# Gated-delta recurrence: inverse and its turned form in PSUM banks of their own, and row sums of exponents in two split passes

## The chip, the cores and the metric

The kernel runs on one core of a Trainium2 chip. The metric is the device time of one execution in microseconds (us), the median of three runs.

## What is computed

One layer of a streaming encoder with three groups of mixing heads (window attention, gated delta rule, stick-breaking attention) and a feed-forward part, for a prompt of 2048 tokens and eight samples of 16 tokens. What matters here is the gated delta rule, six heads of width 64, in chunks of 64 tokens:

```python
gc = jnp.cumsum(g, axis=-1)
decay = jnp.exp(jnp.where(causal, gc[..., :, None] - gc[..., None, :], NEG))
kb = k * beta
lower = jnp.where(strict, jnp.einsum("...id,...jd->...ij", kb, k) * decay, 0.0)
rhs = jnp.concatenate([v * beta, kb * jnp.exp(gc)[..., None]], -1)
sol = lax.linalg.triangular_solve(lower + jnp.eye(chunk), rhs, left_side=True, lower=True, unit_diagonal=True)
u, w = sol[..., :dv], sol[..., dv:]
intra = jnp.where(causal, jnp.einsum("...id,...jd->...ij", q, k) * decay, 0.0)
...
v_new = u_i - w_i @ s
o = (q_i * jnp.exp(gc_i)) @ s + a_i @ v_new
s = s * jnp.exp(g_last) + (k_i * jnp.exp(g_last - gc_i)).T @ v_new
```

## The kernel before

The program runs its stages one after the other: front, window attention, recurrence (stage_delta), stick-breaking attention, mixing, feed-forward. Each stage gives every engine one instruction stream, written out by hand in its order, and engines meet only at semaphores. The order of the calls in each engine's loop is therefore the order of the work; nothing reorders it.

stage_delta handles 17 tiles of 128 tokens: tile 0 holds the samples, tiles 1 to 16 the prompt, two chunks each on the two halves of the partitions. The loop variable k counts turns. In turn k tile k is inverted, tile k-1 is solved and applied to the state, tile k+1 is prepared, and the output of tile k-2 is turned and stored. SP loads tiles four ahead (load), and stores.

The triangular solve is an inverse by doubling. POOL multiplies mats by level masks (mask_L, first_masks, later_masks) into L, and writes X_1, the inverse at the first level. PE's first_inverse(k) brings it into PSUM by products with the identity, once straight (a = 0) and once turned (a = 1); ps_X has two banks, and each holds three heads, both forms side by side. inverse_copied takes bank 0 to SBUF on DVE and bank 1 on ACT. Each level l then has lower_times_inverse (L times X into ps_Y, copied to Y by ACT in product_copied) and add_to_inverse (X times Y, added in ps_X). Levels run to 5, for tile 0 to 3. The last level needs only the turned form, XT, which solved() uses. Between these steps the PE stream has work of the other tiles: solved, kv_rows, from_state, into_state, exponents, products, norms_and_sums, turn_out.

Preparation of tile k+1: norms_and_sums on PE (twelve matmuls with two columns and a few with six), factor_logs on DVE (small 128x6 operations, result fac_log), factors on ACT, log_diag on POOL (identity times a row of fac_log, into diag), kv_rows on PE with scale_kv on DVE, then per half exponents on PE: seq_sum times diag, 384 columns of fp32, plus a mask product in bf16; weights on ACT takes the exponential, products on PE and matrices on DVE give mats.

DVE's loop in turn k: inverse_copied(k, 0), factor_logs(k+1), inverse_copied(k, 1), scale_kv(k+1), squares_summed, inverse_copied(k, 2), state_updated, normalised, decays(k+2), inverse_copied(k, 3), matrices(k+1, 0), inverse_copied(k, 4), state_updated, matrices(k+1, 1), inverse_copied(k, 5), output(k-1). POOL's: later_masks(k), soften(k+2), log_diag(k+1), gates, square(k+2), in turn 0 sample_operands, first_masks(k+1), squared_and_gated(k-1). ACT's begins: inverse_copied(k, 0), product_copied(k, 1), wT_copied(k-1), factors(k+1), inverse_copied(k, 1).

Names and tensors of the trace: d_inverse is X, d_inverse_T is XT, d_inverse_first X_1, d_LX is Y, d_minus_L is L, d_log_diag is diag, ps_d_prepared is ps_P. All products of the doubling have line L2623, that of the helper quadrants. An fp32 matmul stands as two records, so twelve matmuls of a quadrants call over three heads (or one call over six) show as x12 (or x24).

At the start of the stage DVE sets three large tiles to zero, then signals blank_ready, on which SP loads the sample states and after them load(2) and load(3). Before the loop, DVE runs decays(0), factor_logs(0), scale_kv(0), matrices(0, 0) and (0, 1), decays(1).

## Time and profile before

| what | value |
| --- | --- |
| median of 3 runs | 3658.67 us (3653.52 to 3665.99) |
| the profiled execution | 3662.05 us |
| its span | 3660.6 us |
| mean granted clock of TensorE | 0.959 |
| PE busy | 3386.8 us, 93% |
| PEld busy | 3029.3 us, 83% |
| DVE busy | 2121.3 us, 58% |
| ACT busy | 1451.0 us, 40% |
| POOL busy | 390.7 us, 11% |

The profiled execution is one run with the hardware profiler on, and its span is the time from its first to its last instruction. The shares are averages over stages with different limits, so the stage of the change must be looked at by itself: it lies in slices 10 to 16 of the page's 40. PE is TensorE, PEld its weight loads, DVE VectorE, ACT ScalarE, POOL GpSimd, SP SyncE. A granted clock of 1.00 is 2.4 GHz and 0.5 is 1.2 GHz.

### The profile page before, as it was taken

What the parts mean: (1) busy time and instruction counts of PE and PEld (TensorE: products, weight loads), DVE (VectorE), ACT (ScalarE), POOL (GpSimd) and SP (SyncE); (2) the same over time, 40 slices, a digit from 0 to 9 for tenths busy, and PEclk for the clock granted to TensorE, in tenths of its full rate; (3) what the DMA queues carried; (4) which work ended last, traced back from release to release, by engine and by line L of the source; (5) the groups of instructions that cost most, each with busy time, mean ns of one, the idle gap of its engine ahead of it and who ended that gap; (6) DMA issues with size and microseconds to landing.
All of it is one profiled execution on the core that took longest, in us unless ns stands there. A gap on an engine that the chain in (4) does not pass through costs nothing. (4 is left out here: it accounts for less than half of the span.)

```text
span 3660.6 us, 68507 instructions
## 1 busy us (share of the span) xinstructions
PE 3386.8 (93%) x27409; PEld 3029.3 (83%) x27409; DVE 2121.3 (58%) x3584; ACT 1451.0 (40%) x2716; POOL 390.7 (11%) x582
## 2 busy tenths in 40 slices
PE   7999999876999996996599599999999999999997
PEld 7899999854888884664488599899899899899895
DVE  2656556664444444773488465575575575575695
ACT  2434444452344443663334243343343343343353
POOL 0000000022444441000023100000000000000000
PEclk8999999987999998998899799999999999999999
DMA  7677756632011103007666645455455455455464
GB/s 221 176 223 224 224 171 188 189 116 64 22 35 36 45 18 115 7 7 269 203 200 214 191 127 161 128 161 161 128 161 161 128 161 161 128 161 149 143 192 129
DMA packets 706413, 521.55 MB, mean 142 GB/s; under 512 B 64649, under 2 KB 650616, under 8 KB 706044
## 3 DMA queue, kind: packets, MB, share of 16 engines
q1 hardware_dynamic: 659400, 429.25, 39.8%
q0 software_dynamic: 26576, 70.12, 5.6%
q10 hardware_dynamic: 20128, 17.83, 1.6%
q8 instruction: 222, 3.64, 0.4%
q14 instruction: 87, 0.70, 0.1%
HBM read 432.11 MB, written 86.05 MB: 142 GB/s over the span
## 5 line engine op out<-in xcount | busy, mean ns | idle before, releaser
L1219 PE MATMUL ps_gate_up<-h2T_group_high,w_gate_up_high 128*128 128x384 f32 (+1 forms) x2112 | 689.5, 326 | 22.1 <-DVE w_gate_up_low L1315 16.2
L1220 PE MATMUL ps_gate_up<-h2T_group_low,w_gate_up_high 128*128 128x384 f32 (+1 forms) x2112 | 688.6, 326 | 0.0
L1221 PE MATMUL ps_gate_up<-h2T_group_high,w_gate_up_low 128*128 128x384 f32 (+1 forms) x2112 | 688.6, 326 | 0.0
L1219 PEld LDWEIGHTS ps_gate_up<-h2T_group_high,w_gate_up_high 128*128 128x128 f32 x2112 | 398.8, 189 | 24.7 <-issue 24.6
L1220 PEld LDWEIGHTS ps_gate_up<-h2T_group_low,w_gate_up_high 128*128 128x128 f32 x2112 | 398.8, 189 | 0.0
L1221 PEld LDWEIGHTS ps_gate_up<-h2T_group_high,w_gate_up_low 128*128 128x128 f32 x2112 | 398.8, 189 | 0.0
L1315 DVE TENSOR_TENSOR w_gate_up_low<-w_gate_up,w_gate_up_high 128x1024 fp32r<-128x1024 f32 x264 | 322.3, 1222 | 62.2 <-ACT w_gate_up_high L1253 51.7
L1321 DVE TENSOR_TENSOR w_down_low<-w_down_ring,w_down_high 128x512 fp32r<-128x512 f32 x264 | 182.3, 693 | 290.6 <-ACT w_down_high L1259 290.5
L1253 ACT ACTIVATE w_gate_up_high<-w_gate_up 128x1024 fp32r<-128x1024 f32 x264 | 279.3, 1058 | 159.2 <-PE ps_gate_up L1221 135.1
L1259 ACT ACTIVATE w_down_high<-w_down_ring 128x512 fp32r<-128x512 f32 x264 | 166.0, 631 | 331.4 <-PE ps_down L1231 169.3
L433 PE MATMUL ps_feature<-hT_high,w_in_high 128*128 128x384 f32 (+1 forms) x816 | 271.6, 333 | 9.7 <-DVE hT_low L607 8.4
L435 PE MATMUL ps_feature<-hT_high,w_in_low 128*128 128x384 f32 (+1 forms) x816 | 266.6, 327 | 0.0
L434 PE MATMUL ps_feature<-hT_low,w_in_high 128*128 128x384 f32 (+1 forms) x816 | 266.5, 327 | 0.0
L581 DVE TENSOR_TENSOR w_in_low<-w_in_ring,w_in_high 128x1024 fp32r<-128x1024 f32 (+1 forms) x150 | 170.1, 1140 | 125.2 <-ACT w_in_high L497 125.2
L1231 PE MATMUL ps_down<-w_down_high,hidden_high 128*128 128x512 f32 x506 | 199.6, 394 | 4.4 <-DVE w_down_low L1321 2.0
L497 ACT ACTIVATE w_in_high<-w_in_ring 128x1024 fp32r<-128x1024 f32 (+1 forms) x150 | 148.5, 990 | 137.3 <-PE ps_token L453 91.7
L1231 PE MATMUL ps_down<-w_down_low,hidden_high 128*128 128x512 f32 x506 | 197.2, 390 | 0.0
L1231 PE MATMUL ps_down<-w_down_high,hidden_low 128*128 128x512 f32 x506 | 197.2, 390 | 0.0
L1270 ACT ACTIVATE gate_raw<-ps_gate_up 128x384 f32<-128x384 f32 (+1 forms) x132 | 60.0, 455 | 319.5 <-PE ps_gate_up L1221 319.5
L433 PEld LDWEIGHTS ps_feature<-hT_high,w_in_high 128*128 128x128 f32 x816 | 154.5, 189 | 14.3 <-issue 12.4
L1358 DVE SCALAR_TENSOR_TENSOR gated_down<-gate_raw,ffn_taps,gated_down 128x384 f32<-128x384 f32 (+1 forms) x264 | 151.7, 575 | 21.2 <-issue 1.7
L434 PEld LDWEIGHTS ps_feature<-hT_low,w_in_high 128*128 128x128 f32 x816 | 154.5, 189 | 0.0
(437 smaller groups left out, 6681.3 us busy)
## 6 DMA issues: line engine op xcount, KB each, us to landing
w_gate_up<-in_w_gate SPq DMA_DIRECT2D x132, 512.0 KB, 3.7
w_gate_up<-in_w_up SPq DMA_DIRECT2D x132, 512.0 KB, 3.7
w_down_ring<-in_w_down SPq DMA_DIRECT2D x264, 256.0 KB, 2.8
w_in_ring<-in_w_in SPq DMA_DIRECT2D x84, 512.0 KB, 4.2
w_ada_ring<-in_w_ada SPq DMA_DIRECT2D x48, 512.0 KB, 5.3
s_ck_rows<-in_cache_c_k SPq DMA_DIRECT2D x32, 512.0 KB, 7.8
s_cv_rows<-in_cache_c_v SPq DMA_DIRECT2D x32, 512.0 KB, 7.5
d_convT<-scratch_convT SPq DMA_DIRECT2D x17, 576.0 KB, 4.3
```

Of the source, the lines that this page charges most:

```text
L433: pe.matmul(out, high[:, cols], h_high, start=(k == 0), stop=False)
L434: pe.matmul(out, high[:, cols], h_low, start=False, stop=False)
L435: last = pe.matmul(out, low[:, cols], h_high, start=False, stop=(k == DC - 1))
L581: dve.tensor_tensor(w_low[:, u % SPLIT, 0:width], w[:, u % RAW, 0:width], w_high[:, u % SPLIT, 0:width].bitcast(F32), ALU.subtract).then_i ...
L1219: pe.matmul(out, w_high, h_high, start=(k == 0), stop=False)
L1220: pe.matmul(out, w_high, h_low, start=False, stop=False)
L1221: last = pe.matmul(out, w_low, h_high, start=False, stop=(k == DC - 1))
L1231: last = pe.matmul(down_bank(half, t), h[:, c, tok], w[:, j % WR], start=(c == 0 and part == 0), stop=(c == FC - 1 and part == 2))
L1253: act.activation(flat(wgu_high[:, c % 2, j]), flat(wgu[:, c % 2, j]), ACT.Identity).then_inc(s[f"high_ready{j}"], 1)
L1259: act.activation(wd_high[:, j % WR], wd[:, j % WD], ACT.Identity).then_inc(s["wd_high_ready"], 1)
L1315: dve.tensor_tensor(flat(wgu_low[:, c % 2, j]), flat(wgu[:, c % 2, j]), flat(wgu_high[:, c % 2, j]).bitcast(F32), ALU.subtract).then_inc(s ...
L1321: dve.tensor_tensor(wd_low[:, j % WR], wd[:, j % WD], wd_high[:, j % WR].bitcast(F32), ALU.subtract).then_inc(s["wd_split"], 1)
```

## The change

Each bank of ps_X now holds one form for all six heads: bank 0 the inverse, which DVE copies to X, and bank 1 the turned form, which ACT copies to X_T (XT at the last level). PE waits for DVE's copy alone before L times X. For tiles from 1 on the first doubling issues only the products that give the straight form; the turned form is X_1 itself, which ACT copies into bank 1 (inverse_begun) and which add_to_inverse reads at level 1. DVE's copy at the last level is gone. The row sums of the exponents run as two fp32r products over high and low parts: ACT rounds two rows of fac_log (rows_rounded), DVE subtracts (row_low, at the end of factor_logs), POOL makes both diagonals (eight operations instead of four). DVE's three large memsets move from the stage's begin to behind decays(1); SP waits for load(0) before load(1).

```diff
--- before.py
+++ after.py
@@ -2385,13 +2385,14 @@
     GATE = {0: slice(0, H), 1: slice(H, 2 * H)}
-    BETA, KBE, KD, QG = range(4)
+    QG, KBE, BETA, KD = range(4)
...
         half_size = lambda name, shape: ctx.enter_context(nc.sbuf_tensor(name, shape, BF16))
+        sb_r = lambda name, shape: ctx.enter_context(nc.sbuf_tensor(name, shape, F32R))
...
         decay = sb("d_decay", [P, LATE, DEC_B, J])
-        diag = sb("d_log_diag", [P, H, 2, C])
+        row_high, row_low = sb_r("d_row_logs_high", [P, 2, H]), sb("d_row_logs_low", [P, 2, H])
+        diag_high, diag_low = (sb_r(f"d_log_diag_{n}", [P, H, 2, C]) for n in ("high", "low"))
+        seq_sum_r = sb_r("d_seq_sum", [P, P])
...
         X_1 = sb("d_inverse_first", [P, H, C])
-        X, XT = sb("d_inverse", [P, H, 2, C]), sb("d_inverse_T", [P, H, C])
+        X, X_T, XT = (sb(f"d_inverse{n}", [P, H, C]) for n in ("", "_turning", "_T"))
...
                              "squares_ready soft_in_ready soft_ready g_ready norms_done logs_ready sums_done fac_log_ready "
-                             "fac_ready diag_ready kv_done kv_ready G_done wgt_ready qk_done mats_ready L_ready X_1_ready "
+                             "fac_ready row_high_ready rows_split diag_ready kv_done kv_ready G_done wgt_ready qk_done mats_ready L_ready X_1_ready base_ready "
...
         Y_base = lambda n: 0 if n == 0 else 3 + 5 * (n - 1)
-        X_base = lambda n: Y_base(n) + n
...
             load(0)
+            sp.wait_ge(loaded[0], 32)
...
             def log_diag(n):
-                pool.wait_ge(s["fac_log_ready"], n + 1)
+                pool.wait_ge(s["rows_split"], n + 1)
...
                 for half in range(2):
-                    for a, f in enumerate((QG, KBE)):
-                        row = fac_log[:, f].rearrange("p (j a) -> p a j", a=2)[:, half]
-                        last = pool.tensor_tensor(diag[:, halves[half], a, :], ident[:].unsqueeze(1).to_broadcast([P, J, C]),
-                                                  row.unsqueeze(2).to_broadcast([P, J, C]), ALU.mult)
+                    for diag, rows in ((diag_high, row_high[:].bitcast(F32)), (diag_low, row_low[:])):
+                        for a in range(2):
+                            row = rows[:, a].rearrange("p (j a) -> p a j", a=2)[:, half]
+                            last = pool.tensor_tensor(diag[:, halves[half], a, :], ident[:].unsqueeze(1).to_broadcast([P, J, C]),
+                                                      row.unsqueeze(2).to_broadcast([P, J, C]), ALU.mult)
...
                 if n:
-                    for half in range(2):
-                        pool.wait_ge(s[f"Z_done{half}"], X_base(n - 1) + 1)
+                    pool.wait_ge(s["Z_done1"], Y_base(n - 1) + 1)
...
             def sample_operands():
+                pool.wait_ge(s["blank_ready"], 1)
...
             square(1)
-            pool.wait_ge(s["blank_ready"], 1)
...
         def _(pe):
-            def quadrants(outs, lhs, rhs, heads, first, stop):
-                for i in heads:
+            def quadrants(bank, lhs, rhs, first):
+                for i in range(H):
...
                         r = rows_of[c]
-                        last = pe.matmul(outs(r, i), lhs(r, i), rhs(r, i), start=first and i == heads[0], stop=stop,
+                        last = pe.matmul(bank[r, i * C:(i + 1) * C], lhs(r, i), rhs(r, i), start=first and i == 0, stop=True,
...
                 return last
-
-            def heads_of(half):
-                return range(half * J, half * J + J)
-
-            def inverse_at(a):
-                return lambda r, i: ps_X[r, i // J, i % J * 2 * C + a * C:i % J * 2 * C + (a + 1) * C]
...
                     pe.wait_ge(s["mats_ready"], 2 * n + 1)
-                pe.matmul(ps_P[:, 0:W], seq_sum[:, 0, :], flat(diag[:, halves[half]]), start=True, stop=True)
+                pe.matmul(ps_P[:, 0:W], seq_sum_r[:], flat(diag_high[:, halves[half]]), start=True, stop=False)
+                pe.matmul(ps_P[:, 0:W], seq_sum_r[:], flat(diag_low[:, halves[half]]), start=False, stop=True)
...
                 pe.wait_ge(s["X_1_ready"], n + 1)
-                for half in range(2):
-                    if n:
-                        pe.wait_ge(s[f"X_ready{half}"], X_base(n))
-                    quadrants(inverse_at(1), lambda r, i: K["ident"][r, r], lambda r, i: X_1[r, i, :], heads_of(half), True, True)
-                    quadrants(inverse_at(0), lambda r, i: X_1[r, i, :], lambda r, i: K["ident"][r, r], heads_of(half), False, True
-                              ).then_inc(s[f"Z_done{half}"], 1)
+                if n:
+                    pe.wait_ge(s["X_ready0"], Y_base(n))
+                quadrants(ps_X[:, 0], lambda r, i: X_1[r, i, :], lambda r, i: K["ident"][r, r], True).then_inc(s["Z_done0"], 1)
+                if n == 0:
+                    quadrants(ps_X[:, 1], lambda r, i: K["ident"][r, r], lambda r, i: X_1[r, i, :], True)
...
                 pe.wait_ge(s["L_ready"], Y_base(n) + l)
-                for half in range(2):
-                    pe.wait_ge(s[f"X_ready{half}"], X_base(n) + l)
-                    last = quadrants(lambda r, i: ps_Y[r, i * C:(i + 1) * C], lambda r, i: L[r, l, i, :],
-                                     lambda r, i: X[r, i, 0, :], heads_of(half), half == 0, True)
-                last.then_inc(s["Y_done"], 1)
+                pe.wait_ge(s["X_ready0"], Y_base(n) + l)
+                quadrants(ps_Y, lambda r, i: L[r, l, i, :], lambda r, i: X[r, i, :], True).then_inc(s["Y_done"], 1)
...
             def add_to_inverse(n, l):
+                turned = X_1 if l == 1 else X_T
                 pe.wait_ge(s["Y_ready"], Y_base(n) + l)
-                for half in range(2):
-                    if l < last_level(n):
-                        quadrants(inverse_at(0), lambda r, i: X[r, i, 1, :], lambda r, i: Y[r, i, :], heads_of(half), False, True)
-                    quadrants(inverse_at(1), lambda r, i: Y[r, i, :], lambda r, i: X[r, i, 1, :], heads_of(half), False, True
-                              ).then_inc(s[f"Z_done{half}"], 1)
+                if l == 1:
+                    if n:
+                        pe.wait_ge(s["base_ready"], n)
+                else:
+                    pe.wait_ge(s["X_ready1"], Y_base(n) + l - 1)
+                if l < last_level(n):
+                    quadrants(ps_X[:, 0], lambda r, i: turned[r, i, :], lambda r, i: Y[r, i, :], False).then_inc(s["Z_done0"], 1)
+                quadrants(ps_X[:, 1], lambda r, i: Y[r, i, :], lambda r, i: turned[r, i, :], False).then_inc(s["Z_done1"], 1)
...
             def solved(n):
-                for half in range(2):
-                    pe.wait_ge(s[f"X_ready{half}"], X_base(n) + last_level(n) + 1)
+                pe.wait_ge(s["X_ready1"], Y_base(n) + last_level(n))
...
 
+            def rows_rounded(n):
+                act.wait_ge(s["fac_log_ready"], n + 1)
+                act.activation(row_high[:], fac_log[:, QG:KBE + 1], ACT.Identity).then_inc(s["row_high_ready"], 1)
+
+            def inverse_begun(n):
+                act.wait_ge(s["X_1_ready"], n + 1)
+                act.wait_ge(s["X_ready1"], Y_base(n))
+                act.activation(ps_X[:, 1, 0:W], X_1[:].rearrange("p h c -> p (h c)"), ACT.Identity).then_inc(s["base_ready"], 1)
+
             def inverse_copied(n, l):
-                act.wait_ge(s["Z_done1"], X_base(n) + l + 1)
-                if l < last_level(n):
-                    last = act.activation(flat(X[:, halves[1]]), ps_X[:, 1, 0:W], ACT.Identity)
-                else:
-                    last = act.activation(XT[:, halves[1]], ps_X[:, 1, 0:W].rearrange("p (h a c) -> p h a c", a=2, c=C)[:, :, 1],
-                                          ACT.Identity)
-                last.then_inc(s["X_ready1"], 1)
+                act.wait_ge(s["Z_done1"], Y_base(n) + l)
+                dst = X_T if l < last_level(n) else XT
+                act.activation(dst[:].rearrange("p h c -> p (h c)"), ps_X[:, 1, 0:W], ACT.Identity).then_inc(s["X_ready1"], 1)
...
             norm_logs(0)
+            rows_rounded(0)
...
                 solving, preparing = exists(k - 1) and not sample(k - 1), exists(k + 1)
-                if exists(k):
-                    inverse_copied(k, 0)
+                if exists(k) and k:
+                    inverse_begun(k)
...
                 if preparing:
+                    rows_rounded(k + 1)
...
         def _(dve):
-            for t in (s_state, s_wT, s_qT):
-                last = dve.memset(t[:], 0.0)
             dve.memset(sums[:], 0.0)
-            dve.drain()
-            dve.sem_inc(s["blank_ready"], 1)
+            dve.tensor_copy(seq_sum_r[:], seq_sum[:, 0])
...
                 dve.tensor_tensor(fac_log[:, KD], minus_gc[:], whole, ALU.add).then_inc(s["fac_log_ready"], 1)
+                dve.wait_ge(s["row_high_ready"], n + 1)
+                dve.tensor_tensor(row_low[:], fac_log[:, QG:KBE + 1], row_high[:].bitcast(F32), ALU.subtract
+                                  ).then_inc(s["rows_split"], 1)
...
             def inverse_copied(n, l):
-                dve.wait_ge(s["Z_done0"], X_base(n) + l + 1)
-                if l < last_level(n):
-                    last = dve.tensor_copy(flat(X[:, halves[0]]), ps_X[:, 0, 0:W])
-                else:
-                    last = dve.tensor_copy(XT[:, halves[0]], ps_X[:, 0, 0:W].rearrange("p (h a c) -> p h a c", a=2, c=C)[:, :, 1])
-                last.then_inc(s["X_ready0"], 1)
+                dve.wait_ge(s["Z_done0"], Y_base(n) + l + 1)
+                dve.tensor_copy(X[:].rearrange("p h c -> p (h c)"), ps_X[:, 0, 0:W]).then_inc(s["X_ready0"], 1)
...
             decays(1)
+            for t in (s_state, s_wT, s_qT):
+                last = dve.memset(t[:], 0.0)
+            last.then_inc(s["blank_ready"], 1)
...
                     decays(k + 2)
-                if 3 in inverting:
+                if 3 in inverting and not sample(k):
...
                     matrices(k + 1, 1)
-                if 5 in inverting:
-                    inverse_copied(k, 5)
...
```

## Rows read from the trace of the kernel before

**Rows 1.** Busy time and records by engine, clock, DMA: steady part of the stage.

```profile
990.00:1384.00 394.00, 385.80 (x7729) 342.21 (x7728) 177.39 (x429) 164.51 (x479) 178.78 (x230) 0.95 0.12 33
```

**Rows 2.** Timeline of POOL, d_inverse_first: start us, us, engine, line, operation.

```profile
990.44 0.99 POOL L2559 TENSOR_TENSOR d_inverse_first<-d_minus_L,delta_ident 128x384 f32<-128x384 f32 x1 [0.20 <-issue]
...
1218.32 0.99 POOL L2559 TENSOR_TENSOR d_inverse_first<-d_minus_L,delta_ident 128x384 f32<-128x384 f32 x1 [0.20 <-issue]
...
1245.36 0.99 POOL L2559 TENSOR_TENSOR d_inverse_first<-d_minus_L,delta_ident 128x384 f32<-128x384 f32 x1 [0.20 <-issue]
...
1275.10 0.99 POOL L2559 TENSOR_TENSOR d_inverse_first<-d_minus_L,delta_ident 128x384 f32<-128x384 f32 x1 [0.20 <-issue]
```

**Rows 3.** Timeline of PE, from the first doubling of a full-clock turn to level 2.

```profile
1107.95 0.56 PE L2623 MATMUL ps_d_inverse<-d_inverse_first,const_ident 64*64 64x64 f32 x12
...
1109.62 1.04 PE L2623 MATMUL ps_d_LX<-d_inverse,d_minus_L 64*64 64x64 f32 x21
...
1111.61 0.52 PE L2623 MATMUL ps_d_inverse<-d_LX,d_inverse 64*64 64x64 f32 x12
...
1113.91 0.91 PE L2623 MATMUL ps_d_LX<-d_inverse,d_minus_L 64*64 64x64 f32 x24
```

**Rows 4.** Timeline of DVE, the same stretch.

```profile
1108.92 0.56 DVE L3094 COPY d_inverse<-ps_d_inverse 128x384 f32<-128x384 f32 x1 [0.22 <-PE ps_d_inverse L2623]
...
1110.58 0.96 DVE L3071 TENSOR_TENSOR d_minus_gc<-d_norm_logs,d_sums 128x6 f32<-128x6 f32 x1
...
1112.52 0.56 DVE L3094 COPY d_inverse<-ps_d_inverse 128x384 f32<-128x384 f32 x1
```

**Rows 5.** Timeline of POOL, the same turn.

```profile
1104.50 0.99 POOL L2549 TENSOR_TENSOR d_minus_L<-d_matrices,delta_level_T 128x384 f32<-128x384 f32 x1 [14.19 <-DVE d_matrices L3088]
...
1110.52 3.88 POOL L2549 TENSOR_TENSOR d_minus_L<-d_matrices,delta_level_T 128x384 f32<-128x384 f32 x4
```

**Rows 6.** Timeline of PE: row sums, fp32r products of another stage, an uncovered copy.

```profile
1092.32 0.86 PE L2623 MATMUL ps_d_LX<-d_inverse,d_minus_L 64*64 64x64 f32 x23
1093.11 0.91 PE L2668 MATMUL ps_d_prepared<-d_log_diag,delta_seq_sum 128*128 128x384 f32 x2
1093.86 0.33 PE L2669 MATMUL ps_d_prepared<-d_expo_mask_half,d_ident_half 128*128 128x384 bf16 x1
1094.12 0.56 PE L2623 MATMUL ps_d_inverse<-d_LX,d_inverse 64*64 64x64 f32 x12
...
2200.05 0.33 PE L1219 MATMUL ps_gate_up<-h2T_group_high,w_gate_up_high 128*128 128x384 f32 x1
2200.22 0.33 PE L1220 MATMUL ps_gate_up<-h2T_group_low,w_gate_up_high 128*128 128x384 f32 x1
...
900.68 0.92 PE L2623 MATMUL ps_d_LX<-d_inverse,d_minus_L 64*64 64x64 f32 x24
...
902.19 0.56 PE L2623 MATMUL ps_d_inverse<-d_LX,d_inverse 64*64 64x64 f32 x12 [0.59 <-ACT d_LX L2925]
```

**Rows 7.** Timeline of DVE, PE and POOL in the first turns; last row: DMA issues, to landing.

```profile
862.76 2.62 DVE L3026 MEMSET d_s_wT<- 128x3072 f32 x1 [0.59 <-issue]
...
870.45 2.69 PE L2638 MATMUL ps_d_prepared<-delta_in_seq,d_squares 128*128 128x2 f32 x12 [15.96 <-DVE d_expo_mask_half L3032]
...
867.56 0.20 POOL L2531 TENSOR_TENSOR d_soft_in<-d_zero,d_zba 128x6 f32<-128x6 f32 x1 [6.08 <-DMA d_norm_w<-in_b_norm_w]
...
875.89 1.91 POOL L2542 TENSOR_TENSOR d_log_diag<-delta_ident,d_factor_logs 128x192 f32<-128x192 f32 x4 [4.02 <-DVE d_factor_logs L3074]
...
894.72 0.20 POOL L2531 TENSOR_TENSOR d_soft_in<-d_zero,d_zba 128x6 f32<-128x6 f32 x1
...
895.16 0.56 DVE L3094 COPY d_inverse<-ps_d_inverse 128x384 f32<-128x384 f32 x1 [3.17 <-PE ps_d_inverse L2623]
...
d_convT<-scratch_convT SPq DMA_DIRECT2D x4, 576.0 KB, 6.3
...
921.18 0.91 PE L2623 MATMUL ps_d_inverse<-d_inverse_first,const_ident 64*64 64x64 f32 x12
```


## Prediction

> **What bounds the kernel now.** I read the page first and then the stages. The change lies in one stage, the gated-delta recurrence, which runs from about 859 to 1405 us. In the middle of it, the steady part, TensorE is busy 385.80 of 394 us and its mean granted clock is 0.95 [rows 1]. VectorE and ScalarE are under half busy there. So TensorE's queue sets the time, and the other engines matter where its next instruction waits for them. A busy TensorE here also covers short gaps, since the ends of matmuls are modelled, so I go by start times, not by busy time.
>
> One 128-token tile is one turn of the loop. The POOL instruction that writes d_inverse_first marks it. From 1218.32 to 1245.36 a turn takes 27.04 us. The next takes 29.74, and ten turns from 990.44 take 284.66, or 28.47 each [rows 2]. The difference of 1.43 us a turn is time at half clock (1.2 instead of 2.4 GHz); where TensorE runs the two-column norm matmuls just before, little streams through it. So there are two things to sum: the turn at full clock, and what the clock takes.
>
> **First doubling.** Before, first_inverse issues four groups of 12 matmul records, and now two (the identity products that wrote the turned form go). A group costs about 0.35 us: VectorE's copy starts when two groups from 1107.95 have started and the last record of 0.22 has ended, at 1108.92 (0.75 for two). So 0.70 us of TensorE's work goes. But the next step is a dependence. That copy starts 0.97 after the first matmul, and L times X begins at 1109.62 [rows 3, 4]. After the change the same 24 records come first, so VectorE starts at the same 0.97. Its copy of 0.56 and a hand-over of about 0.06 let L times X start at 1.6 instead of 1.67. What is left is that L times X no longer waits half-way for ScalarE's copy; the row at 1109.62 runs 1.04 us with 21 records, the one of level 3 at 1092.32 0.86 with 23 [rows 3, 6], so 0.18 and the 0.07, 0.25 us in all. So of 0.70 us of work removed, 0.45 becomes an idle gap, and add_to_inverse, at 1111.61 before, can start about 0.25 earlier.
>
> **The new wait behind it.** That 0.25 must pass VectorE. Its order is copy of X, the small factor_logs operations, copy of X for level 1. The last row shows that second copy at 1112.52 with no idle time before it: VectorE is late there already, TensorE's L times X of level 2 following at 1113.91 [rows 3, 4]. The change puts into that chain a round trip: fac_log to ScalarE (rows_rounded), back to VectorE (row_low), then only the copy. Queued behind row_low are the copy of X for level 1 and scale_kv; TensorE's level 2 waits for the copy. The trace of before has no such operation on ScalarE; the nearest row of that size is POOL's of 0.20 at 894.72 [rows 7], so with two hand-overs of 0.05 the trip costs 0.3, plus row_low (0.2 by the same row if undisturbed). But a VectorE subtraction of two SBUF tiles of this size takes 0.96 at 1110.58, while POOL runs mask products of 0.97 each (3.88 for four from 1110.52), and ends at 1111.54, about when the first of them does [rows 4, 5]. So row_low costs 0.2 to 1.0.
>
> The Trainium skill's page "SBUF — State Buffer", section "Who interferes with whom", says that a VectorE instruction with two SBUF inputs and a GpSimd instruction that reads SBUF exclude each other for a whole instruction. By that rule row_low costs a full product; without it the step would cost 0.5. The rows side with the rule.
>
> POOL itself moves. VectorE no longer copies at the last level, so output() need not wait for that level, and POOL goes from its first masks at 1104.50 straight on. Three products of 0.97, a pause between them, and the two 384-column products of the output are some 4.9 us, so the four later products start near 1109.4 instead of 1110.52 [rows 5] (an estimate). If VectorE's first small operation just gets in, row_low ends at about 1113.25, the copy at 1113.8, and level 2 starts at 1113.9: no gain, no loss. If it doesn't, the chain is one product later and level 2 starts at 1114.4: 0.5 lost. I take the middle, +0.25, in full-clock turns. In half-clock turns TensorE is slower than this chain and keeps what it is given: 0.4 (the first group of products takes twice the time, the idle gap doesn't). With eight and seven turns: +2.0 and -2.8 us.
>
> **Row sums.** One fp32 pass over 384 columns is two records, 0.75 us from start to start (1093.11 to 1093.86). An fp32r matmul of this shape starts 0.17 after the one before (2200.05, 2200.22) [rows 6]. Two of them and the change of form cost 0.35 to 0.4. So TensorE saves 0.35 to 0.4 per half. How much arrives depends on what the row sums covered: ScalarE's copy of LX. With nothing between, L times X at 900.68 is followed by add_to_inverse at 902.19: 1.51 us. Level 3 takes 1.80 now (1092.32 to 1094.12) [rows 6], so it can only fall by 0.29. Level 4's row sums start later behind L times X, for they wait for matrices(), so nearly all of TensorE's saving arrives there, an estimated 0.32. Sum 0.61 a turn (0.3 if ScalarE is late, 0.8 with no cover lost) for 15 turns: -9.0 us (-4.5 to -12).
>
> log_diag becomes eight POOL products instead of four, +1.91 us by its row [rows 7]. In a steady turn they follow the masks that end at 1114.4, so they end by 1118.8, and the next row sums start at 1093.11 + 27.04 = 1120.15; POOL has 14.19 idle us before 1104.50 to take the rest [rows 5, 6]. If that cover were gone each turn would pay up to 1.9. The added ScalarE copy of X_1 into PSUM (no row of before; about the 0.56 of VectorE's copy of that size, 0.3 to 0.7) runs between the mix copy and the LX copy, where ScalarE idles; it has no price. The full-width last copy on ScalarE is needed only by solved(), after L times X: no price.
>
> **The start.** Before, the three blanking memsets hold VectorE for 3.2 us each (2.62 and 0.59 idle, twice), TensorE waits for the masks that VectorE makes after them until 870.45, and POOL's first work at 867.56 waits for the norm row's load [rows 7]. With the memsets gone TensorE can follow the squares, 1.0 us earlier; with load(1) held back the row may land earlier too. That gain g is 1 to 4; I take 2. log_diag(0), 1.91 at 875.89, doubles and gets the round trip, 2.4 more; the key and value rows cover part of it, so +1.0 (0 to 2.4). The two row sums run at half clock there, where the 0.75 is 1.50 and the new pair 0.7 to 0.8: 0.7 less each. So matrices come 2.4 earlier. But the memsets now stand between decays(1) and the first copy of X, at 895.16 after 3.17 idle, so decays(1) ends at 891.99 [rows 7]. 891.99 less 2.4 plus 9.0 (three of 2.62, two pauses) is 898.6: +3.4. The same signal releases SP: state loads and load(2) are queued behind it, and POOL's soften(2), at 894.72 before, must wait for load(2). With 6.3 us from issue to landing [rows 7] and the state loads ahead, that is about 906. Behind it stand log_diag(1), square, sample_operands and the first masks of tile 1, whose doubling starts at 921.18 now. POOL is some 11 us late there. It had idle time of about that length later in the turn (it is busy 178.78 of 394 us in the steady part [rows 1]), so I don't add the two: the +3.4 less 0.6 for what the row sums save in this turn, +2.8 (-1 to +6).
>
> **The clock.** Nothing in the norms changes, and which turns are hit depends on how they fall. With an idle gap right behind and fewer columns streamed, I expect somewhat more of it: +3 us, from -5 to +19 (all 15 turns like the worst one, 2.70 instead of 1.43). The last two turns, without preparation, give -0.4.
>
> **Sum:** -9.0 +2.0 -2.8 +2.8 +3.0 -0.4 = -4.4 us. The profiled execution took 3662.05 (span 3660.6), 3.4 above the median of 3658.67, which is within the spread of the runs; against it the sum gives 3657.7, against the median 3654.3.
>
> **The rivals.**
> 1. The gain arrives in full (g near 4, VectorE's chain gets in before the masks, 0.8 a turn from the row sums): -12 for the row sums, -2.8 -2 for the doubling, -1 for the start, +0 clock: 3641. For it: the 0.8 and 0.70 us of work removed a turn are real, and TensorE bounds. Against: ScalarE's copy at 902.19. Chance 0.22.
> 2. The round trip takes the lock's place: each turn loses 0.5 and, at the start, load(2) holds POOL to the full (+6): 3654.3 + 2 + 3.2 + 2.8, about 3662. It decides if row_low ends after 1113.4 on the clock of that turn. For it: VectorE has no idle time before 1112.52. Chance 0.25.
> 3. Slower: the clock falls in every turn, between norms and first doubling, at 2.70 a turn. That is 19 us more than now in place of the 3: 3670. It exceeds the gain from about six more turns hit. For it: the gap is put just behind the thinnest stretch. Against: the transposes of turn_out stand between them. Chance 0.13. The Trainium skill's page "TensorE: Matmul & The Clock Gate", section "HAM oscillation — how this bites in real kernels", tells of idle gaps that send the clock down turn after turn; it would make this rival likelier, and the rows so far show falls only behind the norms.
>
> **How the numbers follow.** My forecast, 3654.3, has chance 0.40. A measurement of this kernel can tell about 0.3%, 11 us, from no change. Forecast and rival 2 fall inside that, rival 1 and 3 mostly outside. Faster by over 0.3%: 0.24; within: 0.61; slower: 0.15. The range takes in rival 1's and rival 3's near parts: 3640 to 3669.
>
> **What would show it.** First doubling to level 2, 5.96 us before (1107.95 to 1113.91): 5.7 to 6.5 after, with an idle gap of about 0.9 us on TensorE released by VectorE's copy. Row sums 0.4 instead of 0.75, and add_to_inverse of level 3 at 1.5 us behind L times X. A full-clock turn of 26.4 (26.0 to 26.9). The copy of X for level 0 of tile 0 near 898.6, POOL's soften(2) waiting for a load. If a full-clock turn is 27 or more, the round trip is mis-sized; if it is below 26, the covers are. If the stage's mean clock falls below 0.93, rival 3 holds.

## The result, and the profile after

The changed kernel takes 3695.21 us (median of 4 runs, 3694.63 to 3697.7) against 3662.33 for the kernel before on the same chip. The ratio is 1.0086, with a 95% interval from 1.0068 to 1.0103: slower by 0.9%, where 3654.3 was forecast, and outside the range of 3640 to 3669.

Its profiled execution has a span of 3693.9 us, 33.3 more than before. I cut both spans at four points that both traces have: the POOL instructions that write d_inverse_first for tiles 3 and 16, and the first gate product (L1219) of the last stage, the feed-forward network.

| stretch | before, us | after, us | difference |
| --- | --- | --- | --- |
| start of the span to tile 3 | 990.4 | 999.4 | +9.0 |
| tile 3 to tile 16 (13 turns) | 367.5 | 378.3 | +10.8 |
| tile 16 to the first gate product | 707.7 | 708.4 | +0.7 |
| first gate product to the end | 1594.9 | 1607.7 | +12.8 |

Three of the four grew by about the same. The last of them is a stage in which no line was changed. I take them in turn.

**The turns.** The windows of the steady part and of three parts of one turn (columns: window, its length, busy us and records of PE, PEld, DVE, ACT and POOL, granted clock, DMA share, GB/s):

```profile
1000.00:1384.00 384.00, 369.06 (x7012) 334.09 (x7013) 158.42 (x414) 158.42 (x471) 198.99 (x277) 0.88 0.11 33
...
1023.30:1026.72 3.42, 3.31 (x59) 3.20 (x57) 2.04 (x5) 0.49 (x1) 1.39 (x2) 1.00 0.71 205
1026.72:1036.96 10.24, 9.49 (x160) 8.84 (x161) 3.11 (x10) 2.95 (x9) 9.02 (x14) 0.50 0.10 31
1036.96:1053.00 16.04, 15.91 (x313) 14.11 (x310) 6.56 (x17) 8.36 (x26) 4.59 (x7) 1.00 0.02 4
```

The mean clock is 0.88 where it was 0.95 [rows 1], and in this turn TensorE is granted 1.2 GHz for 10.24 us. Here are the beginnings of four turns on POOL, from tile 3 on; the one with 10.24 us is the second:

```profile
999.43 0.99 POOL L2562 TENSOR_TENSOR d_inverse_first<-d_minus_L,delta_ident 128x384 f32<-128x384 f32 x1
...
1026.34 1.00 POOL L2562 TENSOR_TENSOR d_inverse_first<-d_minus_L,delta_ident 128x384 f32<-128x384 f32 x1
...
1056.72 1.00 POOL L2562 TENSOR_TENSOR d_inverse_first<-d_minus_L,delta_ident 128x384 f32<-128x384 f32 x1
...
1084.45 1.00 POOL L2562 TENSOR_TENSOR d_inverse_first<-d_minus_L,delta_ident 128x384 f32<-128x384 f32 x1
```

The turn of tile 3 has no stretch at half clock and takes 26.91 us, 0.13 less than its like before [rows 2]. The next two take 30.38 (with 10.2 at half clock) and 27.73 (with 3.4), and so it goes on: all twelve turns after the first fall, seven of them for 10.2 us. Added up, 89 us of the 13 turns are at half clock, against 38 before.

The turn at full clock, on PE, from the first doubling on; the bracket is the idle time before and who ended it:

```profile
1001.75 0.92 PE L2626 MATMUL ps_d_inverse<-const_ident,d_inverse_first 64*64 64x64 f32 x24
1003.42 0.82 PE L2626 MATMUL ps_d_LX<-d_inverse,d_minus_L 64*64 64x64 f32 x21 [0.75 <-DVE d_inverse L3097]
...
1005.19 0.90 PE L2626 MATMUL ps_d_inverse<-d_LX,d_inverse_first 64*64 64x64 f32 x24
...
1007.31 0.52 PE L2656 MATMUL ps_d_prepared<-const_ident,d_convT 128*128 128x128 f32 x3 [0.53 <-DVE d_factor_logs L3075]
...
1008.12 0.91 PE L2626 MATMUL ps_d_LX<-d_inverse,d_minus_L 64*64 64x64 f32 x24
...
1013.57 0.86 PE L2626 MATMUL ps_d_LX<-d_inverse,d_minus_L 64*64 64x64 f32 x23
1014.36 0.44 PE L2665 MATMUL ps_d_prepared<-d_log_diag_high,d_seq_sum 128*128 128x384 f32 x1
...
1014.82 0.34 PE L2667 MATMUL ps_d_prepared<-d_expo_mask_half,d_ident_half 128*128 128x384 bf16 x1
1015.09 0.91 PE L2626 MATMUL ps_d_inverse<-d_LX,d_inverse_turning 64*64 64x64 f32 x24
```

The same turn on DVE and POOL:

```profile
1003.08 3.88 POOL L2553 TENSOR_TENSOR d_minus_L<-d_matrices,delta_level_T 128x384 f32<-128x384 f32 x4
1003.19 0.92 DVE L3064 TENSOR_SCALAR d_norm_logs<-d_norm_logs 128x6 f32<-128x6 f32 x1
...
1006.90 0.15 DVE L3075 TENSOR_TENSOR d_factor_logs<-d_minus_gc,d_sums 128x6 f32<-128x6 f32 x1
1007.33 0.17 DVE L3077 TENSOR_TENSOR d_row_logs_low<-d_factor_logs,d_row_logs_high 128x12 f32<-128x12 f32 x1 [0.28 <-ACT d_row_logs_high L2913]
```

Level 3 goes from L times X to the addition in 1.52 us, 0.28 less than in [rows 6]; level 4 saves about as much. But level 2 comes 6.37 us behind the first doubling, where it came 5.96 behind [rows 3]. TensorE now also waits 0.53 us for factor_logs, ahead of the key and value rows (L2656). VectorE is late with them because its first small operation takes 0.92 us; at nearly the same distance behind the first inverse in the turn that began at 1218.32 it took 0.24, for POOL's four masks began later there.

**The start.** POOL and DVE in the first turns, and PE's row sums of tile 1:

```profile
888.22 2.62 DVE L3147 MEMSET d_s_state<- 128x3072 f32 x1 [0.59 <-issue]
...
897.18 0.49 DVE L3097 COPY d_inverse<-ps_d_inverse 128x384 f32<-128x384 f32 x1
...
908.36 0.20 POOL L2534 TENSOR_TENSOR d_soft_in<-d_zero,d_zba 128x6 f32<-128x6 f32 x1 [17.94 <-DMA d_zba<-scratch_zba]
...
910.55 4.09 POOL L2546 TENSOR_TENSOR d_log_diag_high<-delta_ident,d_row_logs_high 128x192 fp32r<-128x192 f32 x2
910.61 3.67 DVE L3111 TENSOR_TENSOR d_s_faded<-d_s_state,d_decay 128x3072 f32<-128x3072 f32 x1
...
915.63 0.69 PE L2665 MATMUL ps_d_prepared<-d_log_diag_high,d_seq_sum 128*128 128x384 f32 x1 [7.48 <-POOL d_log_diag_low L2546]
...
926.29 1.00 POOL L2562 TENSOR_TENSOR d_inverse_first<-d_minus_L,delta_ident 128x384 f32<-128x384 f32 x1
```

VectorE's memsets hold its first copy of X to 897.18 and, through SP, load(2) as well. POOL waits 17.94 us for that load, log_diag(1) stands behind it, and TensorE waits 7.48 us for log_diag(1). The first inverse of tile 1 comes at 926.29, 7.8 later than before. During that wait the clock falls as well, and stays down for 23.9 us; the fall that began there before lasted 13.7.

**The last stage.** TensorE's waits in 2110 to 3400 us (columns: who, on whom, us in all, times, longest), of the kernel before:

```profile
PE ps_gate_up L1219 <- issue: 5.9, 4, 1.6
```

and of the changed one:

```profile
PE ps_gate_up L1219 <- issue: 11.6, 8, 1.7
```

A turn-back is the jump from the end of a loop's body to its beginning, which I call its head. One turn-back of the loop in the changed kernel, on PE:

```profile
2363.15 0.41 PE L1219 MATMUL ps_gate_up<-h2T_group_high,w_gate_up_high 128*128 128x384 f32 x1 [1.31 <-issue]
2365.92 0.44 PE L1219 MATMUL ps_gate_up<-h2T_group_high,w_gate_up_high 128*128 128x384 f32 x1 [1.49 <-issue]
```

The stage's loop turns back four times in this stretch. Each time TensorE pauses for no other engine ("issue"), once before, and now twice, 2.8 to 3.1 us from start to start, with six matmuls between. Half clock comes behind the double pauses too: 25 us of it between 2110 us and the end, against 9.

### The profile page after: what moved, and what is told of

The parts are those of the page before. It is cut to its first block and busy times, and to the rows that moved or that the text cites. A ratio compares the mean times of both kernels' runs of the same rounds, so it can differ in the third digit from the quotient of the medians.

```text
span 3693.9 us, 67904 instructions
## 1 busy us (share of the span) xinstructions
PE 3400.2 (92%) x27025; PEld 3049.1 (83%) x27025; DVE 2108.7 (57%) x3585; ACT 1453.8 (39%) x2732; POOL 426.9 (12%) x650
## 5 line engine op out<-in xcount | busy, mean ns | idle before, releaser
L1219 PE MATMUL ps_gate_up<-h2T_group_high,w_gate_up_high 128*128 128x384 f32 (+1 forms) x2112 | 693.0, 328 | 27.8 <-DVE w_gate_up_low L1315 16.3
L1219 PEld LDWEIGHTS ps_gate_up<-h2T_group_high,w_gate_up_high 128*128 128x128 f32 x2112 | 401.0, 190 | 31.7 <-issue 31.7
L433 PEld LDWEIGHTS ps_feature<-hT_high,w_in_high 128*128 128x128 f32 x816 | 154.3, 189 | 14.5 <-issue 12.5
```

Source lines behind the costliest of these rows:

```text
L433: pe.matmul(out, high[:, cols], h_high, start=(k == 0), stop=False)
L1219: pe.matmul(out, w_high, h_high, start=(k == 0), stop=False)
```

## Experiments

T13 is the time of the 13 turns from tile 3 to tile 16; "half" is how much of it the granted clock was 0.5; "full turn" is a turn without any, where there is one (two values where such turns differ); "tile 1" the time of its d_inverse_first; "last stage" from the first gate product to the end. All in us, from one profiled execution each; median and ratio are from all runs. e1 to e4, e5 to e8 and e9 to e12 were measured on three chips, where the kernel before took 3666.5, 3667.0 and 3664.9 us, so across these groups the ratio is the column to compare.

| kernel | full turn | T13 | half | tile 1 | last stage | median | ratio to before |
| --- | --- | --- | --- | --- | --- | --- | --- |
| before | 27.0 | 367.5 | 38 | 918.5 | 1594.9 | 3662.3 | |
| changed | 26.9 | 378.3 | 89 | 926.3 | 1607.7 | 3695.2 | 1.0086 [1.0068, 1.0103] |
| e1 | 26.9 | 378.4 | 89 | 929.2 | 1593.4 | 3684.8 | 1.0052 [1.0035, 1.0068] |
| e2 | 27.0 | 364.8 | 31 | 917.9 | 1605.8 | 3677.0 | 1.0032 [1.0023, 1.0042] |
| e3 | none | 361.5 | 51 | 925.8 | 1593.9 | 3665.4 | 1.0000 [0.9990, 1.0010] |
| e4 | 26.6, 27.0 | 363.9 | 44 | 916.4 | 1595.9 | 3663.5 | 0.9987 [0.9976, 0.9998] |
| e5 | none | 380.4 | 96 | 915.0 | 1593.5 | 3673.7 | 1.0020 [1.0007, 1.0033] |
| e6 | 27.4 | 364.3 | 24 | 917.3 | 1595.3 | 3669.8 | 1.0006 [0.9989, 1.0022] |
| e7 | 26.9 | 360.8 | 48 | 915.5 | 1593.1 | 3655.3 | 0.9971 [0.9958, 0.9983] |
| e8 | 26.4, 26.7 | 350.8 | 34 | 927.7 | 1598.6 | 3657.8 | 0.9970 [0.9958, 0.9983] |
| e9 | 26.4 | 350.0 | 34 | 919.7 | 1596.2 | 3648.6 | 0.9952 [0.9935, 0.9969] |
| e10 | 25.7 | 345.4 | 34 | 917.7 | 1595.9 | 3640.4 | 0.9932 [0.9915, 0.9949] |
| e11 | none | 381.9 | 99 | 930.8 | 1593.1 | 3682.9 | 1.0046 [1.0031, 1.0062] |
| e12 | none | 359.3 | 48 | 915.1 | 1593.3 | 3652.4 | 0.9969 [0.9957, 0.9982] |

### The place of a loop in the instruction stream

**e1** pads the changed kernel at the start of the last stage, where TensorE waits for rows anyway; **e2** pads the kernel before.

```
             pe.sem_inc(s["wd_used"], WR)
+            for _ in range(348):
+                pe.wait_ge(s["wd_used"], WR)
```

e2 has 164 in place of 348. Two waits make one instruction: e1's trace has 174 semaphore records more than the changed kernel's.

> The changed kernel, with 174 waits that are already met put into TensorE's instructions at the start of the last stage (the feed-forward network), where TensorE waits 21.9 us for rows anyway. The change takes 686 instructions out of TensorE's stream (768 of matrix products less, 82 waits more, by the compiled programs), and one instruction packet on queue 8 holds 16,384 bytes, 256 instructions by the traces; 174 brings the loop of the last stage back to the place within a packet that it had before. Theory 1 (place of the loop in the instruction stream): the second pause per turn of that loop goes, its clock stays at full, and the last stage is 13 us shorter (from 1653.4 us between 2040.5 and the end to about 1640), about 3682 us in all, and the stage of the recurrence is unchanged. Theory 2 (the two kernels differ in the last stage by something else, such as where data lie in memory): no change, 3695 us, two pauses a turn. Padding costing time by itself: up to 5 us, if it isn't hidden.

> The kernel before, with 82 such waits at the same place, which puts the loop of the last stage where the changed kernel has it within a packet of 256 instructions. Nothing of the change is in it. Theory 1: a second pause a turn, granted clock falls after it, +13 us, about 3675 us. Theory 2: no change, 3662 us.

One turn-back in e2, which has nothing of the change, on PE:

```profile
2342.95 0.41 PE L1221 MATMUL ps_gate_up<-h2T_group_high,w_gate_up_high 128*128 128x384 f32 x1 [1.78 <-issue]
2345.95 0.69 PE L1221 MATMUL ps_gate_up<-h2T_group_high,w_gate_up_high 128*128 128x384 f32 x1 [1.70 <-issue]
```

TensorE's waits in 2110 to 3400 us in e1:

```profile
PE ps_gate_up L1221 <- issue: 6.2, 4, 1.8
```

The DMA queues of the stage of the recurrence, 858 to 1384 us of the kernel before (packets, MB, share), name the packets of instructions:

```profile
q8 instruction: 73, 1.20, 1.0%
```

The same stretch has 18,799 records on TensorE's two queues, 258 a packet, so nearly all of these packets are TensorE's, of 256 instructions each.

Both ways as the first theory had it. In e1 the second pause is gone and the last stage falls by 14.3 us, the median by 10.4, or 14.6 if each is taken against the kernel before beside it. (In that execution the start is 3 us later.) In e2 it appears, with six matmuls between, and the stage grows by 10.9 us, the median by 10.5 over the 3666.5 measured beside it. e10 and e12 stand at a third place, 128 (expected with e10, below), and have one pause. So the last stage's +12.8 comes from where the loop's head lies in TensorE's stream within 256 instructions, and the change moved it by taking 686 away (56,290 records on TensorE's queues before, 55,604 after). That the boundary is crossed between the two pauses is worked out, not seen: twelve matrix instructions and a few waits pass between them, so at 82 the head would lie close before a boundary. The times of the packets fit. In the changed kernel one packet of q8 takes from 2360.41 to 2361.39, and TensorE goes on 1.8 us behind it. The next takes from 2363.44 to 2364.45, and TensorE, idle from 2364.43, goes on 1.5 us behind it. The like packet of the kernel before, from 2343.53 to 2344.51, stops nobody.

The Trainium skill, "Runtime: NRT & Kernel Launch", section "Instruction fetch mechanics", says that an engine's instructions come in blocks of 256, that prefetch is sequential, and that a taken branch whose target is not in the window forces a fetch. The trace agrees, with one pause of 1.2 to 1.8 us a turn-back (up to 2.3 in e6 and e8); that a head at place 82 pays twice is what e1 and e2 add.

### What holds the clock down

**e3** takes the identity products of the turned form back for every tile, behind those of the inverse, and drops ScalarE's copy into PSUM (padded, as all that follow but e4, for the last stage). These twelve products stand as 24 records.

```
                 quadrants(ps_X[:, 0], ..., True).then_inc(s["Z_done0"], 1)
-                if n == 0:
-                    quadrants(ps_X[:, 1], lambda r, i: K["ident"][r, r], lambda r, i: X_1[r, i, :], True)
+                if n:
+                    pe.wait_ge(s["X_ready1"], Y_base(n))
+                quadrants(ps_X[:, 1], lambda r, i: K["ident"][r, r], lambda r, i: X_1[r, i, :], True)
```

> The changed kernel with the turned form's base made by identity products on TensorE again, behind the products of the inverse itself (so they fill the gap in which TensorE waits for VectorE's copy), and ScalarE's copy into PSUM gone; padded as e1 is (190 waits), so it is read against e1. TensorE does 12 products more a turn. Theory 1 (the clock: less streamed around the gap keeps it at half for longer, in every turn): turns fall from an average of 29.1 us between the first inverses of tiles 3 and 16 to about 28.0, some 11 to 15 us less than e1, with turns of 26.5 us that have no stretch at half clock. Theory 2 (the clock falls in every turn for another reason, the shorter row sums or the changed times of the norms): turns stay at 29.1 or become 0.2 longer, 0 to +3 us against e1.

More work for TensorE, and the 13 turns are 16.9 us shorter than e1's. The first doubling of one turn of e3, where the clock falls at 1057.5 us:

```profile
1057.67 1.55 PE L2628 MATMUL ps_d_inverse<-const_ident,d_inverse_first 64*64 64x64 f32 x24
1059.01 1.36 PE L2628 MATMUL ps_d_inverse<-d_inverse_first,const_ident 64*64 64x64 f32 x24
1060.21 0.80 PE L2628 MATMUL ps_d_LX<-d_inverse,d_minus_L 64*64 64x64 f32 x22
```

There is no gap ahead of L times X, and it runs at full clock again. In the changed kernel's turn the same three steps still ran at half clock when the addition of level 1 came, at 1035.5. The expected turns of 26.5 us without a fall didn't come, though: e3 falls in every turn, for 3.4 us in eleven of 13. Half of the theory stands in these runs: with the products behind the norms the clock stays down for a shorter time, and it falls all the same. e3 drops ScalarE's copy too; e8, below, keeps it and fills the gap otherwise.

**e4** and **e6** put one part alone on the kernel before. e4 has the split row sums (in it the rest of the split is stored in fp32r too, in the same shapes); its diff is the change's own, without the lines on X, ps_X, the memsets and SP. e6 has the banks and the first doubling, and none of the split.

> The kernel before with the split row sums alone: row logs rounded on ScalarE and their rest on VectorE, eight products on POOL, two fp32r passes. TensorE's instruction count is that of before, so the last stage must be as before. Theory 1 (row sums save about 0.6 us a turn; the clock's longer stretches come from the removed identity products): 13 turns between the first inverses of tiles 3 and 16 take about 360 us against 367.5, in all 3653 to 3658. Theory 2 (what makes the clock fall in every turn is the row sums, of which a half is gone): 375 us or more for the 13 turns, 3668 to 3675 in all. Round trip through ScalarE costing: turns at full clock stay at 27.0 instead of 26.4.

> The kernel before with the banks of their own and the first doubling without identity products (ScalarE begins the turned form by a copy into PSUM), and nothing else of the change: one fp32 pass of row sums, the start of before. Padded by 174, so the last stage is as before. Theory 1 (taking the identity products away, which leaves TensorE 0.75 us without work behind the norms, is by itself what keeps the clock at half in every turn): the 13 turns take 376 us or more against 367.5, 3672 to 3680 in all, and stretches at half clock of 6.8 to 10.2 us in nearly every turn. Theory 2 (it takes the shorter row sums as well): 365 to 369 us for the 13 turns, 3662 to 3668. Theory 3 (the doubling is worth what the prediction gave it, -2 to +2 us): as theory 2.

e4 rules out its second theory and goes half the way of its first: 3.6 us less in 13 turns where 7.5 was expected, and a median of 3663.5, above the 3653 to 3658. (Its profiled execution is also 6 us short in stages that it doesn't touch.) It has two full turns. In the one of 26.6 both row sums save 0.28 and level 2 comes 0.17 later, with row_low at 0.61 us. In the one of 27.0 the second saving doesn't arrive. The clock falls in eleven of its 13 turns, in eight of the kernel before's, but never for more than 6.8 us. e6 speaks against its first theory, which I held: the gap is there, 0.75 us ahead of L times X, and yet ten of the 13 turns show no fall, T13 is 364.3. But its ten runs spread from 3653.1 to 3678.5 us, more than any other kernel's, so the turns of one execution don't settle how often it falls. What is shown: of stretches of 10.2 us at half clock, e4 has none and e6 one, while the changed kernel, e1 and e5 have seven each and e11 eight.

e6 shows another thing: its full turn is 27.4, longer than before by 0.4, with no round trip in it.

```profile
1194.46 0.82 PE L2624 MATMUL ps_d_LX<-d_inverse,d_minus_L 64*64 64x64 f32 x21 [0.75 <-DVE d_inverse L3092]
...
1198.35 0.52 PE L2654 MATMUL ps_d_prepared<-const_ident,d_convT 128*128 128x128 f32 x3 [0.53 <-DVE d_factor_logs L3073]
```

It is the same 0.53 us of waiting for factor_logs as in the changed kernel. The doubling costs it, not the row sums.

**e8** leaves the products out and moves turn_out(), three transposes that must be done anyway, from ahead of the first doubling into the gap behind it. ScalarE's mix_copied, which reads them, moves with them to before its copy of LX; the lines here are TensorE's.

```
                 if exists(k):
                     first_inverse(k)
+                if exists(k - 3):
+                    turn_out(k - 3)
...
-                if exists(k - 2):
-                    turn_out(k - 2)
+            turn_out(TILES - 1)
```

> The changed kernel, padded, with the three transposes of turn_out moved from ahead of the first doubling into the gap behind it (and ScalarE's mix_copied to before the copy of LX), so that the gap holds work that has to be done anyway, 0.47 us. Theory 1 (what counts for the clock is whether TensorE streams between the norms and L times X): a turn loses 0.4 us of work from its path and its long stretches at half clock; 13 turns in 350 to 362 us against e1's 378.4, 3660 to 3670 in all. Theory 2 (the identity products count because they are more work, not because of where they are; the total streamed a turn is what it was in e1): the stretches at half clock stay as long, 13 turns in 372 to 376. If the moved copy on ScalarE is late for LX, turns gain nothing at full clock either.

TensorE streams just as much a turn as in e1, and T13 is 27.6 us less, with 34 us at half clock instead of 89. Two full turns take 26.4, a third 26.7. The gap is down to 0.27:

```profile
1003.37 0.55 PE L2799 MATMUL ps_d_update<-const_ident,d_out_rows 128*128 128x128 f32 x3
1004.19 0.82 PE L2628 MATMUL ps_d_LX<-d_inverse,d_minus_L 64*64 64x64 f32 x21 [0.27 <-DVE d_inverse L3101]
```

So the place of the work counts, and this repair adds no instruction. **e12** puts the products back on top of it (on e10, so it is read against e10).

> e10 with the identity products of the turned form back as well (12 a turn, 0.35 us of TensorE's time; ScalarE's copy into PSUM gone), so that TensorE has no gap at all behind the first doubling. Theory A (more streamed behind the norms keeps the clock up through most turns; a stretch of 3.4 us at half costs about 0.9 to 1.2 a turn): 13 turns 3 to 8 us shorter than e10's. Theory B (what decides is the thin stretch of the norms ahead, and no work behind it helps further): 13 turns 3 to 5 us longer, by the added work of 0.3 to 0.4 a turn.

T13 grows by 13.9, more than either theory gave: every turn falls, and then the twelve products run wholly or partly at half clock. From their first record to the transposes behind them it is 0.84 to 1.43 us, 15.8 us in the 13 turns. At full clock 24 such records take 0.70 us, and not the 0.35 of the expectation. In e12, with the gap filled, the filler only costs.

### The start

**e5** puts the memsets back to the front; **e7** is e3 with the same edit, **e9** is e8 with it.

```
             for t in (s_state, s_wT, s_qT):
                 last = dve.memset(t[:], 0.0)
             dve.memset(sums[:], 0.0)
+            dve.drain()
+            dve.sem_inc(s["blank_ready"], 1)
```

> The changed kernel, padded as e1 is, with the three memsets of s_state, s_wT and s_qT put back to the front of VectorE's work and POOL's wait for them where it was before; load(1) still waits for load(0). Read against e1. Theory 1 (the late zeroing holds VectorE's first copy of X and, through SP, load(2) and so POOL, for the whole 8 to 9 us by which the start is longer): the first inverse of tile 1 comes at 916 to 919 us instead of 926 to 929, and all that follows with it, 3675 to 3677 in all. Theory 2 (the eight products of log_diag and the round trip delay the start): the first inverse of tile 1 stays after 923, a gain of 0 to 3 us. The 13 turns between tiles 3 and 16 stay at 378 in both.

> e3 (identity products back) with the memsets first as in e5: what is left of the change is the split row sums, banks of their own, and load(1) behind load(0). If the two repairs add up, the turns are e3's 361.5 us for 13 and the start is about 8 us earlier than e3's: about 3657. If the late zeroing and the turns interact (POOL's order, the phase of the clock), 3662 to 3666.

> e8 (transposes of turn_out in the gap) with the memsets first as in e5. If the two repairs add up: the start about 12 us earlier than e8's (its first inverse of tile 1 at 915 to 917 instead of 927.7), the 13 turns at e8's 351 us, 3645 to 3648 in all. If the late zeroing only shifted which turns the clock falls in: 3655.

In e5 the first inverse of tile 1 comes at 914.99, 14 us earlier than e1's, and POOL starts log_diag(1) where it is not held by a load:

```profile
893.79 0.20 POOL L2536 TENSOR_TENSOR d_soft_in<-d_zero,d_zba 128x6 f32<-128x6 f32 x1
...
897.66 0.97 POOL L2548 TENSOR_TENSOR d_log_diag_high<-delta_ident,d_row_logs_high 128x192 fp32r<-128x192 f32 x2 [3.52 <-DVE d_row_logs_low L3083]
```

The median falls by 11 us from e1's. e7 adds the repair of e3, as expected, and is 0.29% faster than the kernel before. e9 adds e8's, and is 9.1 us below e8, or 7.0 if each is taken against the kernel before beside it; its tile 1 comes at 919.7 where 915 to 917 was expected, since tile 0 was late in that execution already (894.6 against e5's 890.0), and the turns are e8's.

### VectorE and POOL

**e10** is e9 with one wait more and its padding cut from 174 instructions to 46, **e11** the changed kernel (padded) with that wait alone.

```
             def later_masks(n):
+                if exists(n + 1):
+                    pool.wait_ge(s["fac_log_ready"], n + 2)
                 for l in range(2, last_level(n) + 1):
```

> e9 with one wait more on POOL: the four mask products of the later levels start only when VectorE's factor_logs of the next tile are done. In the turns at full clock of the changed kernel these products start 3.65 us behind the first inverse (4.70 in the kernel before, where output() held them back), and VectorE's first small subtraction-like operation at 3.76 then takes 0.92 us instead of 0.24, which delays kv_rows and L times X of level 2 by 0.46. Theory 1 (that is the price of VectorE and POOL excluding each other): factor_logs end at about 5.2 us instead of 6.7 behind the first inverse, L times X of level 2 comes 0.4 to 0.6 earlier, a turn at full clock falls from 26.4 to 25.8 to 26.0, 13 turns in 341 to 346 us, 3638 to 3642 in all. Theory 2 (VectorE's times don't depend on POOL, or the delayed masks hold up level 2 or the row sums of the next tile): turns stay at 26.4 or grow. The last stage's loop is here at place 128 within its packet of 256 instructions (0 in the kernel before, 82 in the changed one): six matrix products, 12 instructions, pass between the two pauses of the changed kernel, so there the loop's head stands some 14 to 16 instructions before a packet's end; at 128 it is far from an end, and there should be one pause a turn and 1593 to 1596 us from the first gate product to the end. Two pauses there, and the account of the packet's end is wrong.

> The changed kernel, padded as e1 is, with POOL's wait of e10 and nothing else; read against e1. Theory 1 (VectorE held by POOL costs the turn 0.46 us at full clock): L times X of level 2 comes 8.2 us behind the first inverse instead of 8.7 in a turn at full clock. What the turns gain in all depends on the clock, which falls in every one: 0 to 6 us in 13 turns, 3679 to 3685. Theory 2 (as in e10): nothing, or a loss of up to 5.

The turn at full clock in e10, on DVE, POOL and PE:

```profile
992.73 0.87 PE L2630 MATMUL ps_d_inverse<-const_ident,d_inverse_first 64*64 64x64 f32 x24
...
994.11 0.59 DVE L3074 TENSOR_SCALAR d_norm_logs<-d_norm_logs 128x6 f32<-128x6 f32 x1
...
995.09 0.16 DVE L3082 TENSOR_TENSOR d_minus_gc<-d_norm_logs,d_sums 128x6 f32<-128x6 f32 x1
...
995.64 3.87 POOL L2555 TENSOR_TENSOR d_minus_L<-d_matrices,delta_level_T 128x384 f32<-128x384 f32 x4 [0.96 <-DVE d_factor_logs L3085]
...
998.44 0.92 PE L2630 MATMUL ps_d_LX<-d_inverse,d_minus_L 64*64 64x64 f32 x24
```

Without POOL beside it the operation on d_minus_gc takes 0.16 us, and 0.96 in [rows 4]. Level 2 follows the first doubling after 5.71 us (6.37 in the changed kernel), and a full turn falls by 0.7, to 25.7. e10 is 0.68% faster than the kernel before, the fastest here. And it has one pause a turn-back at its third place, as worked out.

e11 shows the same wait where the clock falls in every turn: nothing. T13 is 3.5 us longer, and the median is 1.9 less, 0.4 less if each is taken against the kernel before beside it. It has no turn at full clock, so the place of level 2 can't be read against its forecast. TensorE's waits of the changed kernel in 1000 to 1384 us show why there is nothing to gain:

```profile
PE ps_d_prepared L2656 <- DVE d_factor_logs L3075: 0.5, 1, 0.5
```

It waits for factor_logs once, in its one turn at full clock. Level 2 comes 12.2 us behind the first inverse in a turn with 10.2 us at half clock, in the changed kernel and in e11 alike, and 9.5 in one with 3.4. The 3.5 us are the turns hit: eight of e11's 13 are of the longer kind, seven of the changed kernel's.

## Why the prediction was wrong, point by point

The sum was -4.4 against the profiled execution, which came out at +33.3. Of the 37.7 us between them 12.8 had no term, 9.5 are the clock, 6.2 the start, 8.5 the work of the turns (-10.2 forecast, 13 times -0.13 measured) and 0.7 the stretch behind tile 16.

- **The sum ended at the stage.** No term stood for the last stage, since nothing in it changes; it gave 12.8 of the 33.3 us. Removed instructions move everything behind them in the stream, and a loop back there pays. e1 and e2 show it. "What is changed" must take in the stream's length.
- **The clock.** The term was +3 (-5 to +19). With full turns of 26.91 and 27.04 us, the clock took 28.5 us of T13 after (378.3 less 349.8) and 16.0 before: +12.5, inside the term's range, 9.5 above its value. Rival 3's mechanism is what happened, falls in every turn but the first, and its sign: the stage's mean clock fell to 0.88. Its price was high (2.70 a turn, measured 2.19) and its chance of 0.13 too low. The step that failed is "the transposes of turn_out stand between them" as an argument against: the clock fell for 10.2 us in seven turns with them there, and in none of e8's, which has them in the gap. I looked only at whether the fall comes, and what changed most is how long it lasts. The Trainium skill's page named there, "TensorE: Matmul & The Clock Gate", section "HAM oscillation — how this bites in real kernels", tells of such falls turn after turn, with long waits for transfers between; the trace agrees on the falls, in twelve turns of 13, though TensorE was idle for no more than 0.8 us at a time here.
- **The start.** The forecast was +2.8 (-1 to +6), measured +9.0. g came out at the top of its range: TensorE's norms began at 866.40 instead of 870.45, and the first inverse of tile 0 came 4.4 us earlier (886.5). X's copy came at 897.2, near the 898.6. What failed is "I don't add the two". POOL's later idle time was there (9.45 us ahead of tile 1's first mask before, 0.34 after), but it lay behind log_diag(1), for which TensorE waits. log_diag(1) began 11.9 us later and ended 16.9 later, for it has four products more (1.9 us) and one of them met VectorE's sample_faded (3.62 us instead of 0.51), which I had not seen. TensorE could cover all but 7.48 us of that. This is the second half of rival 2, load(2) holding POOL to the full. With the memsets in front, in e5, tile 1 comes 3.5 us earlier than in the kernel before, so their place did all of it.
- **First doubling.** The gap was forecast at about 0.9 and is 0.75; first doubling to level 2 at 5.7 to 6.5 and is 6.37, so +0.41 where I had taken +0.25. That the number was inside is luck, for the reason was wrong: row_low took 0.17 us and its round trip 0.28, and both lay beside TensorE's key and value rows. The cost is that POOL's masks start earlier (the prediction had that) and hold factor_logs' first operation for 0.92 us, and the wait that binds is that of the key and value rows, which no step named. e6 has it without the split, e10 takes it away. The Trainium skill, "SBUF — State Buffer", section "Who interferes with whom", covers both: the operations with two SBUF inputs (0.96 us in [rows 4], 0.16 in e10) and, by another of its rules, that a VectorE copy or operation with a constant can take the shared ports too when its operands meet some conditions, which fits the operation of 0.92 us here; the prediction had drawn only on the first.
- **Row sums.** Forecast -0.61 a turn, measured -0.28 at level 3 and -0.27 at level 4, and the same 0.28 twice in e4's turn of 26.6. This step was right, and ScalarE's copy is the bound it was taken for.
- **The full turn.** Forecast 26.4 (26.0 to 26.9), measured 26.91: 27.04 less 0.55, plus 0.41. The 26.4 doesn't follow from the prediction's own terms, which give 26.7 (27.04 less 0.61, plus 0.25). The prediction had 27 as the point from which the round trip would be mis-sized, and here the trip takes 0.28 and row_low 0.17 us beside other work. In e4's turns at full clock row_low takes 0.61, and level 2 comes 0.17 later.

What stays open: why both parts together keep the clock at half for 10 us in more than half of the turns, and either alone does so in one turn or none. e6's spread over its runs shows that single traces can't tell it.

## What to carry to other kernels

Work taken off a bound engine may not be worth its time where the stretch around it thins out. Before removing cheap products from TensorE close to stretches like the two-column norms here, look for needed work to put in their place (e8: 27.6 us in 13 turns, for no more instructions). When an edit frees another engine early, ask whom its next instructions will now meet (POOL's masks and VectorE's factor_logs). And when the instruction count of an engine changes, check the turn-backs of every loop behind: a second pause there can undo the whole gain (12.8 us here), and padding in a stretch where TensorE waits anyway takes it away (174 instructions in e1).

## What the runs showed of the hardware that I had not expected

A loop's turn-back costs TensorE a pause of 1.2 to 1.8 us (2.3 at most, in e6 and e8) once or twice, by where its head lies within 256 instructions: at 0 and 128 once, at 82 twice (places counted against the kernel before). The second pause cost 10.9 (e2) and 14.3 us (e1) over four turn-backs, with the clock's reaction included. In e1 TensorE reached the last stage's first transposes after 32.7 us instead of 21.8, so 174 instructions of already met waits take up to 0.19 us each. The 16 more of e3 made it 34.4, or 0.11 us each. In e1 the next wait, for weights, fell from 12.7 to 2.3 us and took the difference in. And twelve small products placed where the clock has just fallen cost up to twice their 0.70 us, 1.2 a turn on the mean in e12.
